# Two static pairs of experts at the head of a two-layer MoE encoder, and constants multiplied in the waits of each layer's last item

## The chip, the core and the metric

One core of one Trainium2 chip runs the whole program. The metric is the time of one execution on the device in microseconds (us). The engines are PE (TensorE), DVE (VectorE), ACT (ScalarE), POOL (GpSimd) and SP (SyncE, which here only issues DMAs). The rate of PE depends on the clock that is granted to it; in the records it is 1.00 (2.4 GHz) or 0.50 (1.2 GHz), and in between only as a mean over a stretch.

## What is computed

256 tokens of width 1024 go through two layers. Each layer is a mixer (one input projection, three kinds of attention, one output projection) and a mixture of experts: a router picks one of four groups and then two of the eight experts in it. All data is float32.

```python
def reference(x, ...):
    for l in range(DEPTH):                       # DEPTH = 2
        x = x + mixer_sublayer(x, ...)
        x = x + hier_moe(rms_norm(x, norm2_g[l]), ...)
...
    # hier_moe: 32 experts, D_EXPERT = 512, top-2 inside the best group
    e_in = jnp.take_along_axis(e_logits, grp[:, None, None], axis=1)[:, 0]
    top_v, top_i = lax.top_k(e_in, TOP_K_IN_GROUP)
    gate = p_grp[:, None] * jax.nn.softmax(top_v, axis=-1)
...
        return (jax.nn.silu(xb @ w_gate[e]) * (xb @ w_up[e])) @ w_down[e]
```

Every expert has tokens for these inputs, so all 32 experts' weights (6 MB each) are read in both layers. The reference's router, run on these inputs, gives experts 28 to 31 the counts 5, 12, 6, 1 in the first layer and 1, 33, 13, 8 in the second; the largest counts of the others are 54, 42, 35, 31, 28 and 73, 56, 44, 40, 27.

## The kernel before, in words

**The ring.** All large weights pass through `ring`, 16 pieces of 1 MB. `ring_plan` (L86) gives each transfer its piece in advance, one after the other around the ring, and the semaphore value that frees it. A layer's `w_in` takes nine pieces in three groups, `w_out` four, an expert six: two each of gate, up and down. SP issues transfers strictly in the program's order (`piece_in`, L397 to L403) and waits at each one until its piece is free.

**Items.** The 32 experts of a layer are worked on in 11 items of 1, 2 or 4 experts (`KINDS`, in the order of rank; `TIME` is the order in which they are worked on). An item of four gives each expert 32 places of the 128 columns, one of two gives 64, one of one 128. Experts 30 and 31 are `STATIC`: they form the first item whatever the router says. The others are ranked by their number of tokens, and their numbers stand in `order`, which DVE writes (L1514). At every item but the first SP waits for `v_order` (L465). Tokens that don't fit the places of an expert's rank are done again in `rerun`, which loads six pieces more for each.

**An item on PE.** A gather (L847), which makes `xg` from `pick`; six rounds (`round_of`, L878: gate 0 and 1, up 0 and 1, down 0 and 1), each of which frees its pieces at its end by `p_round` or `p_down`; small transposes (L916, L930); and four products back (L947) that DVE adds to `x` (L1617). DVE copies the first half of the gathered rows (`v_xg`, L1561), ACT the second half (`a_xg`, L1144); round 0 needs the first half, round 1 the second. The next item's gather stands between round 3 and round 4. Each layer's last item gathers at its start, and its last transfers are split by rows (`row_in`, L405 to L411), so that its last round (L895) can begin with the first half; the second half waits for `d_last`. Between rounds 4 and 5 of the last item stand seven products of constants (`warm`, L592), whose result nobody reads.

**The head of a layer's experts.** After the logits (L755) PE multiplies constants three times and waits for `v_chosen`. DVE finds the two best experts of each token (L1441 to L1466); PE counts them with `ones` and `tri` (L839); DVE makes the order of the experts (L1496 to L1514), then the places of the static pair (`placings`, L1476 on) and `pick` (L1572), for which the gather waits. After it follow `seatings` (the places of all experts) and `list_again`.

**The mixer.** PE, DVE, ACT and POOL work through a written order of projections, scores, softmax and products. Near the middle PE turns the queries of kind B (L672) after `v_sum`, which DVE writes at L1332; ahead of that DVE reduces the lengths of these queries (L1242) and copies a turned softmax (L1328).

## Time and profile before

| | us |
|---|---|
| median of three runs | 1226.13 (1226.09 to 1231.55) |
| the profiled execution | 1228.69 |
| its span in the trace | 1226.9 |
| mixer of the first layer | 0 to 150 |
| experts of the first layer | 150 to 621 |
| mixer of the second layer | 621 to 755 |
| experts of the second layer | 755 to 1223 |
| busy: PE, DVE, ACT, POOL | 1007.5, 321.6, 169.4, 51.5 |

A row of a timeline begins with its start and its duration in us; then come the engine, the line, the operation, the tiles written and read, and the number of instructions. What stands in brackets is the engine's idle time before it and what ended that. A row of windows has, for each stretch, the busy time of each engine with its number of instructions, the granted clock of PE, the mean busy share of the 16 DMA engines and what they moved in GB/s. A product in float32 shows as two instructions.

### The profile page before, as it was taken

The numbers are of one execution on the slowest core, as the hardware profiler recorded it, in microseconds if no ns is written. First come the engines' busy times: TensorE is split into PE (matmuls) and PEld (weight loads), VectorE is DVE, ScalarE is ACT, GpSimd is POOL, SyncE is SP. The second block draws the span as 40 slices with busy tenths as digits, with TensorE's granted clock in tenths as the row PEclk, the third lists the DMA queues.
The fourth block names the chain that finished last, engine by engine and source line by source line (L and its number), as shares of the span: only waits on it lengthen the run. The fifth ranks groups of instructions, "written<-read, shape, count | busy, mean of one in ns | idle before, by whom it ended". The sixth has DMA issues, their size and how long they took to land.

```text
span 1226.9 us, 14093 instructions
## 1 busy us (share of the span) xinstructions
PE 1007.5 (82%) x5416; PEld 472.2 (38%) x5416; DVE 321.6 (26%) x727; ACT 169.4 (14%) x440; POOL 51.5 (4%) x104
## 2 busy tenths in 40 slices
PE   7999899887969659657799998979889696795667
PEld 4565553333423223213256655434334241241232
DVE  3555542221212102102045555412212021020101
ACT  1343311010100001000024332101011010010000
POOL 1121100000000000000021110000000000000000
PEclk9999999998999888888899998999899897798888
DMA  9942099999999999999988222999999999999996
GB/s 299 371 183 103 1 374 408 421 421 421 421 421 421 422 420 392 406 422 420 412 321 332 100 97 94 399 412 420 421 420 422 421 420 421 421 421 422 420 420 244
DMA packets 74820, 435.84 MB, mean 355 GB/s; under 512 B 12496, under 2 KB 15744, under 8 KB 26624
## 3 DMA queue, kind: packets, MB, share of 16 engines
q1 hardware_dynamic: 74752, 434.92, 87.1%
q8 instruction: 45, 0.74, 0.2%
q14 instruction: 23, 0.19, 0.0%
HBM read 433.84 MB, written 1.05 MB: 354 GB/s over the span
## 4 chain that ended last, share of the span: by engine, by line
PE 52%; DMA 33%; SPq 8%; issue 2%; DVE 2%; ACT 2%; POOL 1%; DVEq 0%; ACTq 0%; POOLq 0%
PE bank L878 23%; DMA ring<-in_w_down 22%; PE bank L624 9%; DMA ring<-in_w_up 7%; SPq L403 6%; PE bank L740 5%; PE bank L947 4%; DMA ring<-in_w_gate 4%; PE bank L847 4%; PE bank L708 1%; PE bank L696 1%; PE bank L686 1%; SPq L411 1%; ACT work L1144 1%; DMA ring<-in_w_in 1%
## 5 line engine op out<-in xcount | busy, mean ns | idle before, releaser
L878 PE MATMUL bank<-ring,work 128*32 128x512 f32 (+2 forms) x3008 | 529.2, 688 | 184.3 <-DMA ring<-in_w_up 68.3
L878 PEld LDWEIGHTS bank<-ring,work 128*32 128x32 f32 (+2 forms) x3008 | 162.3, 134 | 513.6 <-issue 485.4
L624 PE MATMUL bank<-ring,hT 128*128 128x512 f32 (+1 forms) x384 | 130.3, 495 | 1.1 <-DMA ring<-in_w_in 1.1
L847 PE MATMUL bank<-work,h 128*128 128x128 f32 x704 | 92.6, 295 | 11.8 <-issue 6.6
L847 PEld LDWEIGHTS bank<-work,h 128*128 128x128 f32 x704 | 89.4, 209 | 27.3 <-issue 20.2
L1612 DVE COPY work<-bank 128x512 f32<-128x512 f32 x22 | 15.2, 691 | 311.5 <-PE bank L878 278.7
L624 PEld LDWEIGHTS bank<-ring,hT 128*128 128x128 f32 x384 | 72.8, 194 | 49.6 <-issue 42.8
L1604 DVE TENSOR_TENSOR work<-work,bank 128x512 f32<-128x512 f32 x22 | 15.1, 687 | 256.2 <-PE bank L878 256.2
L947 PE MATMUL bank<-work 128*128 128x512 f32 x176 | 82.0, 607 | 0.0
L1617 DVE TENSOR_TENSOR x<-x,bank 128x512 f32<-128x512 f32 x88 | 60.5, 688 | 19.2 <-PE bank L947 19.2
L1144 ACT ACTIVATE work<-bank,gain 128x128 f32<-128x128 f32 x88 | 25.1, 367 | 272.3 <-PE bank L847 272.3
L740 PE MATMUL bank<-ring,h 128*128 128x512 f32 x128 | 59.2, 606 | 0.0
L947 PEld LDWEIGHTS bank<-work 128*128 128x128 f32 x176 | 30.1, 189 | 51.8 <-issue 38.4
L1155 ACT COPY work<-bank 128x256 f32<-128x256 f32 x22 | 8.2, 372 | 290.5 <-PE bank L916 290.5
L1586 DVE TENSOR_TENSOR work<-iota,work 128x512 f32<-128x512 f32 x20 | 13.8, 690 | 126.4 <-PE bank L916 124.9
L1166 ACT COPY work<-bank 128x512 f32<-128x512 f32 x22 | 12.9, 585 | 215.7 <-PE bank L878 186.7
L740 PEld LDWEIGHTS bank<-ring,h 128*128 128x128 f32 x128 | 23.4, 193 | 24.8 <-issue 24.6
L512 POOL TENSOR_TENSOR ms<-ms,eps 128x1 f32<-128x1 f32 x20 | 3.8, 192 | 588.6 <-ACT h L995 500.3
L1342 DVE SCALAR_TENSOR_TENSOR x<-bank,rstd,x 128x512 f32<-128x512 f32 x24 | 18.0, 750 | 33.7 <-PE bank L740 33.7
L1164 ACT COPY work<-bank 128x512 f32<-128x512 f32 x22 | 13.2, 599 | 78.4 <-PE bank L930 78.4
L1561 DVE TENSOR_TENSOR work<-bank,gain 128x512 f32<-128x512 f32 x22 | 15.2, 691 | 31.7 <-PE bank L847 31.7
L515 POOL TENSOR_TENSOR rsh<-msh,mhalf 128x8 f32<-128x8 f32 (+1 forms) x14 | 22.0, 1568 | 1.1
(192 smaller groups left out, 588.5 us busy)
## 6 DMA issues: line engine op xcount, KB each, us to landing
ring<-in_w_gate SPq DMA_DIRECT2D x128, 1024.0 KB, 26.2
ring<-in_w_up SPq DMA_DIRECT2D x128, 1024.0 KB, 26.6
ring<-in_w_down SPq DMA_DIRECT2D x120, 1024.0 KB, 25.3
ring<-in_w_in SPq DMA_DIRECT2D x10, 1536.0 KB, 13.2
ring<-in_w_out SPq DMA_DIRECT2D x8, 1024.0 KB, 17.7
ring<-in_w_down SPq DMA_DIRECT2D x16, 512.0 KB, 20.5
ring<-in_w_in SPq DMA_DIRECT2D x1, 2048.0 KB, 14.7
x<-in_x SPq DMA_DIRECT2D x2, 512.0 KB, 4.6
```

What stands on the lines that cost most here:

```text
L403: sp.dma_start(rows(pos, k), w[:, 0, half * k:half * k + k]).then_inc(landed[pos], 16)
L515: tt(dst, src, spread_to(mhalf, src), ALU.pow).then_inc(g_rstd, 1)
L624: last = matmul(bank[6 + i % 2][:, 0:c1 - c0], hT[:, k, t * P:t * P + P], group_in(l, gi)[:, k, c0:c1], start=(k == 0), stop=(k == KD - 1))
L740: last = matmul(bank[6 + n % 2][:, :], mixed[:, pos0 + c, t * P:t * P + P], rows(pos, 2)[:, c % 2, half * 512:half * 512 + 512], start=(c ...
L847: last = nc.tensor.matmul(bank[k // 4][:, k % 4 * P:k % 4 * P + P], h_kc[:, t, k, :], pick[:, t, :], start=(t == 0), stop=(t == TT - 1))
L878: last = nc.tensor.matmul(bank[b][e * w:e * w + w, :], lhs[:, k, e * w:e * w + w], rows(pos, k_count // 2)[:, kk, n * 512:n * 512 + 512], ...
L947: last = nc.tensor.matmul(bank[2 + n][:, :], pickT[:, t, :], y[:, half * 512:half * 512 + 512], start=True, stop=True)
L1144: last = nc.scalar.mul(xg[:, k, :], bank[1][:, (k - 4) * P:(k - 3) * P], gain2[:, q // NI, k:k + 1])
L1342: stt(xs, bank[6 + n % 2][:, :], rstd[:, c:c + 1], xs, ALU.mult, ALU.add).then_inc(v_x, 1)
L1561: tt(xg[:, 0:4, :], bank[0][:, :].rearrange("p (k s) -> p k s", k=4), wide(gain2[:, q // NI, 0:4], P), ALU.mult).then_inc(v_xg, 1)
L1612: nc.vector.tensor_copy(y[:, 512:1024], bank[7][:, :]).then_inc(v_y, 1)
L1617: tt(xs, xs, bank[2 + n][:, :], ALU.add).then_inc(v_back[n], 1)
```

## The change

1. `STATIC` is 28 to 31, and `KINDS` begins 2, 2, 1, 1: the first two items are static pairs, ahead of any order. `TIME` puts the second pair right behind the first. The two items of one expert come fourth and sixth. The places of each rank move by two with the statics, in `seatings`.
2. `ring_plan` takes the piece that is freed earliest and no longer goes around the ring. Five places beside the ring are laid out (`BESIDE`) in memory that is free while experts are worked on, but `BESIDE_LAST = -1` lets no item use them. For this, tables are moved together, `c_dil` is loaded in each layer, and SP gets waits for these places. `hot` takes over the space of `hotw` and `beats`, so `seatings` counts ranks in two halves.
3. The places of the static pair are made ahead of the order, and PE counts with `tri` first.
4. Round 0 waits for `v_xg` alone, `a_xg` is waited for ahead of round 1.
5. Constants are multiplied (three times at the head of the program, five in place of three behind the logits, 5, 5, 5 and 4 behind rounds 0 to 3 of the last item, two ahead of `d_last`); the seven behind round 4 go.
6. In the mixer, DVE's reduction of the lengths of B's queries is moved behind the copy and `v_sum`. Squares of the last two groups of heads go to other memory, and ACT's waits for `p_sum` there go.

```diff
-STATIC = (30, 31)
-KINDS = [2, 1, 1, 2, 2] + [4] * 6
+STATIC = (28, 29, 30, 31)
+KINDS = [2, 2, 1, 1, 2] + [4] * 6
...
-TIME = [0, 5, 1, 6, 2, 7, 3, 8, 4, 9, 10]
+TIME = [0, 1, 5, 2, 6, 3, 7, 4, 8, 9, 10]
...
+    def take(key, n, done, time, allowed):
+        starts = [i for i in allowed if i + n <= max(allowed) + 1 or n == 1]
+        pos = min(starts, key=lambda i: (max(when[i:i + n]), i))
...
+                if l:
+                    dil_load(l)
...
-                if i:
+                if r0 >= NS:
                     sp.wait_ge(v_order, 2 * l + 1 + (r0 + n > 16))
...
-                warm(7, 3)
+                warm(7, 5)
                 pe.wait_ge(v_chosen, l + 1)
...
                         if kk == 1:
+                            warm(2, 2)
                             pe.wait_ge(d_last, 16 * n_e * (l + 1))
...
                 pe.wait_ge(v_xg, q + 1)
-                pe.wait_ge(a_xg, q + 1)
                 need(pe, v_back[0], q)
                 round_of(0, (2,), xg, p_round)
+                if i == NI - 1:
+                    warm(7, 5)
+                pe.wait_ge(a_xg, q + 1)
                 round_of(1, (2,), xg, p_round)
+                if i == NI - 1:
+                    warm(7, 5)
...
                 round_of(2, (3,), xg, p_round)
+                if i == NI - 1:
+                    warm(7, 5)
                 round_of(3, (3,), xg, p_round)
+                if i == NI - 1:
+                    warm(7, 4)
...
                 round_of(4, (6, 7), hidT, p_round)
-                if i == NI - 1:
-                    warm(2, 7)
...
                 projected(l, 11)
-                head_lengths(l, "qB")
                 softmax_copied(l, 4)
                 sum_raised(l, 1)
+                head_lengths(l, "qB")
...
-                expert_order(l)
                 placings(l)
                 seated(nc.vector.tensor_copy(rgc[:, 0:TT], rg[:, 0:TT, e0:e0 + 2]))
                 tt(pair_hot, ...).then_inc(v_pick, 1)
+                expert_order(l)
                 expert_order_rest(l)
...
-                seated(tt(hotw, hot, wide(weights, P), ALU.mult))
-                tt(pickw, hotw[:, 0:TT], hotw[:, TT:], ALU.add).then_inc(v_pickw, 1)
+                dve.wait_ge(v_pick, q + 1)
+                seated(tt(hot, hot, wide(weights, P), ALU.mult))
+                tt(pickw, hot[:, 0:TT], hot[:, TT:], ALU.add).then_inc(v_pickw, 1)
```

DVE at the head of the experts, before; `bank` holds PE's counts, `order` the experts' numbers, and `work` is, among others, `pick`:

```order
L1496 SCALAR_TENSOR_TENSOR work<-bank,order_key 128x32 [waits p_rank]
L1508 MAX work<-work 1x8 [waits v_step]
L1509 MATCH_REPLACE work<-work 1x32 [waits v_step]
L1510 MAX work<-work 1x8 [waits v_step]
L1514 TENSOR_SCALAR order<-work 1x16 [waits v_step]
L1476 SCALAR_TENSOR_TENSOR work<-bank,work 128x2x32 [waits v_chosen,p_rank]
L1478 TENSOR_SCALAR rg<-work 128x64 [waits v_step]
L1571 COPY rgc<-rg 128x4 [waits v_step]
L1572 TENSOR_TENSOR work<-iota,rgc 128x256 [waits v_istep]
```

and the same place now:

```order
L1528 SCALAR_TENSOR_TENSOR work<-bank,work 128x2x32 [waits v_chosen,p_rank]
L1530 TENSOR_SCALAR rg<-work 128x64 [waits v_step]
L1623 COPY rgc<-rg 128x4 [waits v_step]
L1624 TENSOR_TENSOR work<-iota,rgc 128x256 [waits v_istep]
L1548 SCALAR_TENSOR_TENSOR work<-bank,order_key 128x32 [waits p_rank]
L1560 MAX work<-work 1x8 [waits v_step]
```

The five instructions that make the order now stand behind the write of `pick`.

PE at the end of the last item of the second layer, from round 3 on, before (`ring,work 32x512` are the rounds, `dil,ident` the constants, `work 128x512` the products back):

```order
L878 MATMUL bank<-ring,work 32x512 [waits landed0,landed1,landed15,landed14]
L878 MATMUL bank<-ring,work 32x512 x15
L930 MATMUL bank<-ident,work 128x128 [waits v_back2,v_hid]
L930 MATMUL bank<-ident,work 128x128 x3
L878 MATMUL bank<-ring,work 32x512 [waits landed3,landed2,landed4,v_y,landed5,a_y,a_hidT]
L878 MATMUL bank<-ring,work 32x512 x15
L592 MATMUL bank<-dil,ident 128x384 x7
L895 MATMUL bank<-ring,work 32x512 [waits landed8,landed9,landed7,landed6]
L895 MATMUL bank<-ring,work 32x512 x7
L895 MATMUL bank<-ring,work 32x512 [waits d_last]
L895 MATMUL bank<-ring,work 32x512 x7
L947 MATMUL bank<-work 128x512 [waits a_y,a_pickT]
```

and now:

```order
L923 MATMUL bank<-ring,work 32x512 [waits landed10,landed11,landed5,landed4]
L923 MATMUL bank<-ring,work 32x512 x15
L631 MATMUL bank<-ident 128x384 x4
L984 MATMUL bank<-ident,work 128x128 [waits v_back2,v_hid]
L984 MATMUL bank<-ident,work 128x128 x3
L923 MATMUL bank<-ring,work 32x512 [waits landed6,landed0,landed12,v_y,landed13,a_y,a_hidT]
L923 MATMUL bank<-ring,work 32x512 x15
L941 MATMUL bank<-ring,work 32x512 [waits landed8,landed14,landed7,landed1]
L941 MATMUL bank<-ring,work 32x512 x7
L631 MATMUL bank<-ident 128x384 x2
L941 MATMUL bank<-ring,work 32x512 [waits d_last]
L941 MATMUL bank<-ring,work 32x512 x7
```

The seven products of constants behind round 4 are gone; four stand behind round 3 and two ahead of the second half of the last round.

In the first layer the ring is filled, before and now, by the static pair's 12 transfers, of which nine wait for the projections' `p_proj`. The four pieces left are those of `w_out`, freed by `p_out` 4, 4, 8 and 12. Before, they go to the gate 0 weights of an item of four, behind `v_order`; now to gate 0 and gate 1 of the second static pair. The next transfer waits for `p_round` 1, the end of the first item's round 0, in both kernels.

## Rows read from the trace of the kernel before

**Rows 1.** The page: granted clock in tenths and DMA rate, 40 equal slices

```profile
PEclk9999999998999888888899998999899897798888
GB/s 299 371 183 103 1 374 408 421 421 421 421 421 421 422 420 392 406 422 420 412 321 332 100 97 94 399 412 420 421 420 422 421 420 421 421 421 422 420 420 244
```

**Rows 2.** SP's waits: us in total, times, longest

```profile
SPq L465 <- DVE order L1514: 107.1, 2, 54.4
```

**Rows 3.** Windows of the first layer: engines, clock, DMA share, GB/s

```profile
110.00:150.00 40.00, 38.75 (x193) 22.70 (x191) 21.10 (x59) 15.48 (x35) 4.90 (x13) 1.00 0.00 1
...
165.00:170.00 5.00, 5.00 (x24) 1.73 (x22) 4.37 (x23) 1.14 (x2) 0.00 (x0) 1.00 0.82 280
...
185.00:190.00 5.00, 5.00 (x22) 1.65 (x17) 1.15 (x2) 0.58 (x1) 0.00 (x0) 1.00 0.98 387
...
195.00:200.00 5.00, 5.00 (x50) 1.53 (x46) 0.51 (x1) 0.51 (x2) 0.00 (x0) 1.00 0.98 377
```

**Rows 4.** Timeline of PE, first item and start of the second, first layer

```profile
153.69 6.38 PE L847 MATMUL bank<-work,h 128*128 128x128 f32 x32 [2.38 <-DVE work L1572]
161.34 7.09 PE L878 MATMUL bank<-ring,work 128*64 128x512 f32 x32 [1.28 <-issue]
...
175.75 3.84 PE L847 MATMUL bank<-work,h 128*128 128x128 f32 x32
...
192.01 7.07 PE L878 MATMUL bank<-ring,work 128*32 128x512 f32 x64
```

**Rows 5.** Timeline of all engines, head of the first layer's experts

```profile
151.42 0.18 DVE L1496 SCALAR_TENSOR_TENSOR work<-bank,order_key 128x32 f32<-128x32 f32 x1
...
152.43 0.22 DVE L1476 SCALAR_TENSOR_TENSOR work<-bank,work 128x64 f32<-128x64 f32 x1
...
160.10 1.14 ACT L1144 ACTIVATE work<-bank,gain 128x128 f32<-128x128 f32 x4 [8.27 <-PE bank L847]
```

**Rows 6.** Timeline of PE, head of the second layer's experts

```profile
752.30 3.50 PE L592 MATMUL bank<-dil,ident 128*128 128x384 f32 x6
...
758.61 5.44 PE L847 MATMUL bank<-work,h 128*128 128x128 f32 x32 [2.31 <-issue]
```

**Rows 7.** Timeline around the turn of B's queries, both layers

```profile
97.03 1.09 PE L696 MATMUL bank<-ident,work 128*128 128x128 f32 x8 [0.19 <-DVE work L1321]
...
99.06 0.69 DVE L1242 TENSOR_REDUCE msh<-work 128x8 f32<-128x512 f32 x1 [1.69 <-ACT work L1021]
...
100.55 0.63 PE L672 MATMUL bank<-ident,h 128*128 128x128 f32 x4 [2.09 <-DVE ms L1332]
...
707.10 0.63 PE L672 MATMUL bank<-ident,h 128*128 128x128 f32 x4 [2.09 <-DVE ms L1332]
```

**Rows 8.** Windows in which the clock fell

```profile
753.10:756.40 3.30, 3.02 (x10) 1.16 (x8) 2.96 (x24) 1.36 (x1) 0.00 (x0) 0.50 0.00 0
...
101.60:104.80 3.20, 3.20 (x17) 2.04 (x16) 0.07 (x1) 1.10 (x4) 1.31 (x4) 0.55 1.00 425
```

**Rows 9.** Timeline of PE, end of the second layer

```profile
1194.71 6.32 PE L878 MATMUL bank<-ring,work 128*32 128x512 f32 x32 [6.33 <-DMA ring<-in_w_up]
...
1204.64 6.47 PE L878 MATMUL bank<-ring,work 128*32 128x512 f32 x32 [1.98 <-DMA ring<-in_w_down]
1211.04 4.78 PE L592 MATMUL bank<-dil,ident 128*128 128x384 f32 x14
1215.75 3.64 PE L895 MATMUL bank<-ring,work 128*32 128x512 f32 x32
```

**Rows 10.** Window in which the weights' last bytes come

```profile
1214.00:1214.50 0.50, 0.50 (x3) 0.32 (x2) 0.00 (x0) 0.00 (x0) 0.00 (x0) 1.00 0.02 8
```

**Rows 11.** Timeline of PE, last item of the first layer

```profile
574.44 7.07 PE L878 MATMUL bank<-ring,work 128*32 128x512 f32 x64 [1.28 <-issue]
...
603.69 3.64 PE L878 MATMUL bank<-ring,work 128*32 128x512 f32 x32 [1.40 <-DMA ring<-in_w_down]
...
615.42 1.92 PE L895 MATMUL bank<-ring,work 128*32 128x512 f32 x16 [1.53 <-DMA ring<-in_w_down]
```

More of the change, by code:

```diff
@@ L83 @@
 OUT_PIECES = (2, 3, 0, 1)
+BESIDE_FREE = [("p_pv", 8, 24)] * 4 + [("p_logit", 2, 40)]
+TABLES, BIASES, TURNED_ROWS = PIECES + 2, PIECES + 3, PIECES + 4
+BESIDE_LAST = -1
 def ring_plan():
-    at, used, freed, plan = [0], [0] * PIECES, [[] for _ in range(PIECES)], {}
-    def take(key, n, done):
-        if at[0] + n > PIECES:
-            at[0] = 0
-        pos = at[0]
-        before = [f for i in range(pos, pos + n) for f in freed[i]]
+    n_pieces = PIECES + BESIDE
+    used, freed, when, plan = [0] * n_pieces, [None] * n_pieces, [0] * n_pieces, {}
+    def take(key, n, done, time, allowed):
+        starts = [i for i in allowed if i + n <= max(allowed) + 1 or n == 1]
+        pos = min(starts, key=lambda i: (max(when[i:i + n]), i))
         waits = {}
-        for name, value in before:
+        for name, value in filter(None, freed[pos:pos + n]):
             waits[name] = max(value, waits.get(name, 0))
@@ L101, in take @@
             used[i] += i < pos + 2
-            freed[i] = [done]
+            freed[i], when[i] = done, time
         plan[key] = (pos, [used[i] for i in range(pos, pos + n)], sorted(waits.items()))
-        at[0] = (pos + n) % PIECES
+    ring, everything = range(PIECES), range(n_pieces)
     for l in range(LAYERS):
+        t0 = 1000 * l
         for g in range(3):
-            take((l, "in", g), 3, ("p_proj", 12 * l + 4 * g + 4))
+            take((l, "in", g), 3, ("p_proj", 12 * l + 4 * g + 4), t0 + 4 * g + 4, ring)
         for n, j in enumerate(OUT_PIECES):
-            take((l, "out", j), 1, ("p_out", 12 * l + (4, 4, 8, 12)[n]))
+            take((l, "out", j), 1, ("p_out", 12 * l + (4, 4, 8, 12)[n]), t0 + (16, 16, 26, 30)[n], ring)
+        for n, (name, count, time) in enumerate(BESIDE_FREE):
+            freed[PIECES + n], when[PIECES + n] = (name, (l + 1) * count), t0 + time
         for i, it in enumerate(TIME):
@@ L115, in ring_plan @@
                 for e in range(KINDS[it]):
-                    take((l, i, r, e), 1, done)
+                    take((l, i, r, e), 1, done, t0 + 100 + 10 * i + r, everything if i <= BESIDE_LAST else ring)
+        for n in range(BESIDE):
+            plan[l, "beside", PIECES + n] = freed[PIECES + n]
     return plan
@@ L215, in encoder @@
                    "kB": proj[:, :, 256:512], "qB": proj[:, :, 256:512]}
[L216 to L220 removed]
+        staged = [queries.rearrange("p j s -> p (j s)"), hT_flat]
+        flip = [s[0:GRID, 0:P] for s in staged]
+        windows = [s[0:GRID, P:P + 1000] for s in staged]
+        gain_rows = [s[0:3 * KD, 1128:1128 + P] for s in staged]
+        beside = [work[:, 0:PIECE], work[:, PIECE:2 * PIECE], tables[:], biased[:], hT_flat]
+        o = [2 * PIECE]
         def carve(n):
@@ L257, in encoder @@
             sem("d_" + n) for n in ("ident", "gains", "rel", "mask", "rope", "qkg", "route", "gain2", "const", "out"))
-        d_last = sem("d_last")
-        landed = [sem(f"landed{i}") for i in range(PIECES)]
+        d_last, d_dil = sem("d_last"), sem("d_dil")
+        landed = [sem(f"landed{i}") for i in range(PIECES + BESIDE)]
         p_gains, p_xT, p_proj, p_flip, p_turn, p_s, p_pt, p_pv, p_sum, p_out, p_yT, p_logit, p_rank = (
@@ L290, in rows @@
         def rows(pos, k):
-            return ring[:, pos * PIECE:(pos + 1) * PIECE].rearrange("p (k c) -> p k c", k=k)
+            piece = ring[:, pos * PIECE:(pos + 1) * PIECE] if pos < PIECES else beside[pos - PIECES]
+            return piece.rearrange("p (k c) -> p k c", k=k)
         def rooted(l, name):
@@ L361, in spread, with kept_no_more, dil_load @@
                 return src.partition_broadcast(P).rearrange("p a c -> p (a c)")
+            def kept_no_more(l, pos):
+                name, value = PLAN[l, "beside", pos]
+                sp.wait_ge(frees[name], value)
+            def dil_load(l):
+                if l:
+                    kept_no_more(l - 1, TABLES)
+                sp.dma_start(dil, a["c_dil"]).then_inc(d_dil, 16)
             def staged_loads(l):
+                kept_no_more(l - 1, TURNED_ROWS)
                 gain_loads(l)
@@ L1428, in mixers @@
                 if l == 0:
[L1429 removed]
+                    dve.wait_ge(d_const, 64)
                     router_constants()
```

104 lines of the change are left out of this document (57 added, 47 removed).

## The prediction

> **What bounds the kernel now.** I read the page's slices first [rows 1]: in each layer the stream of weights runs at 421 GB/s for about 450 us, and idle in the second half of the mixer. A piece of 1.049 MB at 421 GB/s takes 2.49 us, so a layer's 192 pieces of experts' weights take 478 us; everything that starts this stream earlier, or shortens what follows its last byte, counts in full, and most of what PE does in between is hidden. SP's own waits come next: 107.1 us go to waiting for the order of the experts, twice some 54 us [rows 2], and that wait looks like what the change removes. The windows then show where the stream leaves gaps: none of it runs from 110 to 150 us, and once running it dips to 280 GB/s at 165 to 170 us and slightly at 185 and 195 [rows 3]. Last come the timelines of PE at the head of the experts and at the end of each layer, which say what the stream and the end wait for.
>
> **The two static pairs.** It is tempting to count four pieces more per layer ahead of the order, 4 x 2.49 = 10.0 us a layer. But the ring holds 16 pieces before and now. Before, 12 lie ready and four are fetched from 153.6 us on, which takes until about 165; the 17th needs the piece that round 0 of the first item frees. That round starts at 161.34 and is half of the two rounds' 7.09 us [rows 4], so it ends at 164.9. The dip at 165 to 170 [rows 3] is this: the stream has caught up with PE and waits for it. Now all 16 lie ready and the stream resumes with the 17th, released by the same round. From there both streams run off the start of round 0, T0. So the head start itself is worth nothing; only a shift of T0 is.
>
> Then the pace. An item costs PE 192.01 - 161.34 = 30.7 us whether it has two experts or four [rows 4], since 64 or 32 columns of several experts run side by side. The first static pair frees two pieces at T0 + 3.6, 7.1, 11.0, 14.5, 23.6 and 27.1, the second at 30.7 more each. The stream needs 2.49 us a piece: 24 pieces take 59.8 us, and with a gap each where the pair of pieces comes late (behind the products back of either item) I get 61.5, a loss of 1.7 us. Before, the item of four follows, and the two dips behind the 17th piece cost (421 - 387) x 5 / 421 + (421 - 377) x 5 / 421 = 0.9 us [rows 3]. The change loses 0.8 us here in the first layer; in the second I take 0.2, as the same dips were deeper there. PE does not starve: the second pair's up weights are in 10 us after T0, it asks for them after 38. Later the items of one expert free only six pieces in 30.7 us where the stream wants 12, but the item of four before them leaves some 13 pieces free ahead, so they cost nothing.
>
> **T0.** (a) `pick` is written ahead of the order: five DVE instructions from 151.42 to 152.43 leave its path, 1.0 us [rows 5]. They then run during the gather, and end before DVE is wanted for the first half of it. (b) Round 0 no longer waits for ACT's half, 1.28 us of PE's idle time behind the gather [rows 4, 5]; round 1 wants it 3.5 us later, and 1.14 us suffice. (c) The first gather runs at the low clock, 6.38 us where the next takes 3.84 [rows 4]; in the second layer 5.44 [rows 6]. Five products of constants instead of three end at about 151.0, when the counts can start, and (a) shortens the wait behind them to 1.3 us. I take the full clock in the first layer, 2.5 us, with 0 as the other end. In the second the clock had fallen while the products still ran: six instructions took 3.50 us, and the window shows 0.50 with PE busy 3.02 of 3.30 us [rows 6, 8]. There two more products may run at half rate and hold up the counts by up to 2 us, against a gather faster by 1.6: I take +0.6, between -0.5 and +1.6. T0 moves by 1.0 + 1.3 + 2.5 = 4.8 and by 1.0 + 1.3 + 0.6 = 2.9 us. Together with the loss above: 4.0 and 2.7 us.
>
> The Trainium skill ("TensorE: Matmul & The Clock Gate", Part 4: PE-mode transpose) says that transposes don't count as activity for the clock as other products do; the fall behind the turned rows in the second layer agrees, and the first layer, with the same sequence and no fall until 152 us, does not. If the rule held each time, (c) would be the low end in both layers.
>
> **The mixer.** DVE stands idle for 1.69 us, reduces lengths from 99.06, then copies, then writes `v_sum`, and PE stands 2.09 us until 100.55 [rows 7]. The copy can start at 98.1, when PE's turned softmax is out (97.03 + 1.09), so `v_sum` is there at about 98.95 and PE goes on at 99.1: 1.45 us. The same in the second layer [rows 7]. The lengths come out as before, at 99.75, since they wait for ACT until 99.0 in any case. In the first layer the clock then stood at 0.55 for 3.2 us of full work [rows 8], which costs 3.2 x 0.45 = 1.4 us; with the idle time more than halved I count it as won (0 is the other end). PE is busy 38.75 of the 40 us that follow [rows 3], so this reaches T0. ACT's dropped waits were for sums long made: nothing. The three products at the head lie in waits for `x` and `w_in`: 0, at most 0.1 us lost.
>
> **Extra work.** `c_dil` is loaded again in the second layer, 0.8 MB or 1.9 us of a DMA queue that then stands empty for 70 us [rows 1]; SP's new waits are for values long reached. `seatings` has two DVE instructions more, with the next gather 14 us behind T0 and, by my count of DVE's rows, done some 2.5 us ahead of it: hidden, and 1 us late at worst. No expert overflows: 28 to 31 have at most 33 tokens for 64 places, the two largest others 54 and 73 for 128, the next two at most 44 for 64, the rest 28 or fewer for 32.
>
> **The ends of the layers.** At the end of the second layer round 4 starts at 1204.64 at half rate and takes 6.47 us, seven constants 4.7, and only at 1215.75 does the last round of 3.64 us begin; its second half begins at 1217.6 [rows 9]. The last bytes are in at 1214.5 [rows 10]. Now round 4 at full clock ends at 1208.3, the first half and two constants at 1212.7, and the second half can begin as the rows land: 3.1 us won. In the first layer the second half waits for its data at 615.42 already [rows 11]: nothing. For this the item must keep up: from 574.44 - 1.28, four rounds (14.2), 19 constants at 0.68 (12.9), the biases and turns (5) and ACT's copy end at about 606.5, past the 603.69 of before, then round 4, the half and two constants end at 613.5, 2 us ahead of the data [rows 11]. In the second layer the biases are missing, and the slack is some 5 us.
>
> **Sum.** First layer 1.45 + 1.4 + 4.0 = 6.9; second 1.45 + 2.7 + 3.1 = 7.2; together 14 us. The profiled execution would be 1228.7 - 14 = 1214.7; the medians stand 2.6 us below it, so 1226.1 - 14 = 1212 us.
>
> **The rivals.**
> - *The clock stays low.* In (c) and the mixer no clock is won (-2.5, -1.1, -1.4), and at the ends PE still cools in the waits: half rate over the second half and the products back costs up to 3.4 us in each layer, if some 3.4 of their 1.9 + 3.7 us run at it. That leaves 14 - 5 - 6.8 = 2, so 1224. For it: rounds at half rate behind 6.3 us of idle time [rows 9]. Against: the constants fill 3.4 us of such a wait. Here also belongs the skill's rule (same page, Part 1, HAM oscillation) that a stream whose work is shorter than its waits for data cools at every step; rows 9 agree with it for the kernel before.
> - *Slower: the constants become the last item's bound.* If the last item runs at half rate, its 19 constants cost 1.4 us each and its rounds 7, so its chain grows by up to 32 us against a slack of 2 to 5. It decides from some 4 us at half rate in the first layer on; with half of the item slow, 13 us are lost in each layer: 1212 + 26 = 1238. Against: 0.5 came after idle time, and rounds that followed each other ran at 1.00.
> - *The head start counts in full,* if the stream didn't depend on round 0: some 8.6 us a layer on top, 1195. The dip in rows 3 speaks against it.
>
> **How the numbers follow.** Forecast, 1206 to 1219: 0.74. Clock stays low, 1219 to 1226: 0.17. Slower: 0.05. Full head start: 0.04. The range 1205 to 1221 leaves out about 2 in 10. A measurement can tell 0.5%, 6.1 us, from no change: faster (below 1220) 0.80, same 0.14, slower 0.06.
>
> **What would show it.** SP's wait for the order gone, but a wait for PE's first round in its place and a stream that is idle until 3.6 us behind T0; T0 at about 153.5 in the first layer (161.34 - 4.8 - 2.9 from the mixer) and the gather at 3.8 us; PE's idle time at L672's successor down to 0.6 us; round 4 of the last item at 3.6 us; the second half of the last round released by DMA in both layers. It is wrong if the stream resumes earlier than round 0's end, if the gathers still take 5 to 6 us, or if `d_last` is long met when PE comes to it.

## The result, and the profile after

The changed kernel takes 1215.15 us (median of four runs, 1211.87 to 1216.72) against 1226.11 us for the kernel before in the same comparison. The ratio is 0.9896 with a 95% interval of [0.9874, 0.9918], so it is faster by 0.8 to 1.3%. The profiled execution took 1214.72 us with a span of 1212.9, 14.0 less than the span before.

The page of the kernel after: granted clock and DMA rate in 40 slices, to be read against [rows 1].

```profile
PEclk9999899999998988788999999998998989888799
...
GB/s 303 379 180 135 108 306 401 415 421 421 421 422 420 421 423 387 408 422 420 413 325 367 104 173 71 393 403 420 423 420 421 421 421 421 421 420 422 420 420 286
```

The fifth slice shows 108 in place of 1: the second pair's four pieces now come in the middle of the mixer. The next slices show no rate above that of before. SP's waits in the kernel after (in all, times, longest) answer to [rows 2]; the last line is the same wait in the kernel before:

```profile
SPq L439 <- PE bank L923: 271.8, 87, 20.4
...
SPq L439 <- PE bank L780: 79.6, 6, 21.2
...
SPq L403 <- PE bank L878: 209.5, 78, 9.2
```

The 107 us of waiting for the order are gone, and SP waits longer for PE's rounds instead: 271.8 us at L923 against 209.5 us before. Windows of the first layer, T0 (the start of the first item's round 0) being 154.22, answer to [rows 3]; the last line is a row of SP's timeline, its transfers from 157.91 on:

```profile
150.00:155.00 5.00, 4.52 (x36) 3.99 (x38) 4.41 (x26) 0.67 (x3) 0.00 (x0) 1.00 0.00 0
155.00:160.00 5.00, 5.00 (x26) 1.72 (x24) 4.62 (x15) 0.47 (x2) 0.00 (x0) 1.00 0.22 43
160.00:165.00 5.00, 5.00 (x26) 1.55 (x22) 4.35 (x25) 2.25 (x3) 0.00 (x0) 1.00 1.00 423
...
175.00:180.00 5.00, 5.00 (x26) 1.72 (x24) 0.00 (x0) 0.35 (x1) 0.00 (x0) 1.00 1.03 397
...
157.91 4.24 SPq L439 DMA_DIRECT2D ring<-in_w_up  x4
```

The ring is full and the stream stands still until the first item's round 0 ends: the first piece behind it is issued at 157.91, 3.7 us after T0. PE at the head of the program and in the first layer's mixer and head, against [rows 4, 7]:

```profile
10.69 7.14 PE L664 MATMUL bank<-ring,hT 128*128 128x256 f32 x32 [0.31 <-DVE hT L1261]
...
97.09 0.63 PE L712 MATMUL bank<-ident,h 128*128 128x128 f32 x4 [0.60 <-DVE ms L1384]
...
140.50 2.58 PE L795 MATMUL bank<-w_route,hT 128*128 128x36 f32 x16 [0.77 <-ACT hT L1127]
142.90 6.22 PE L631 MATMUL bank<-ident 128*128 128x384 f32 x10
148.95 0.20 PE L884 MATMUL bank<-work,tri 128*128 128x32 bf16 x2
...
150.48 3.81 PE L892 MATMUL bank<-work,h 128*128 128x128 f32 x32 [1.25 <-DVE work L1624]
154.22 7.09 PE L923 MATMUL bank<-ring,work 128*64 128x512 f32 x32
```

T0 moved from 161.34 to 154.22. The gather is at full speed and round 0 follows without idle time. But the constants took 6.22 us for ten instructions, where the same ten take 3.47 in the second layer, and the counts (L884) had to wait for them. The same place of the first layer in the kernel before, where PE waited 1.50 us for DVE ahead of the counts:

```profile
145.56 1.95 PE L755 MATMUL bank<-w_route,hT 128*128 128x36 f32 x16 [0.77 <-ACT hT L1077]
147.34 2.18 PE L592 MATMUL bank<-dil,ident 128*128 128x384 f32 x6
151.01 0.21 PE L839 MATMUL bank<-work,ones 128*128 128x32 bf16 x2 [1.50 <-DVE work L1466]
```

From the start of the last logits to the counts it was 5.45 us before and is 8.45 us now, so 3.0 us are lost there. The second layer, against [rows 6, 7]:

```profile
699.37 0.63 PE L712 MATMUL bank<-ident,h 128*128 128x128 f32 x4 [0.60 <-DVE ms L1384]
...
744.56 3.47 PE L631 MATMUL bank<-ident 128*128 128x384 f32 x10
748.24 0.22 PE L884 MATMUL bank<-work,tri 128*128 128x32 bf16 x2 [0.21 <-DVE work L1518]
749.86 3.81 PE L892 MATMUL bank<-work,h 128*128 128x128 f32 x32 [1.32 <-DVE work L1624]
753.60 7.09 PE L923 MATMUL bank<-ring,work 128*64 128x512 f32 x32
```

The end of the second layer on PE, against [rows 9]:

```profile
1193.47 5.04 PE L923 MATMUL bank<-ring,work 128*32 128x512 f32 x32 [3.05 <-DMA ring<-in_w_down]
1198.59 1.92 PE L941 MATMUL bank<-ring,work 128*32 128x512 f32 x16
1200.45 1.56 PE L631 MATMUL bank<-ident 128*128 128x384 f32 x4
1203.49 1.92 PE L941 MATMUL bank<-ring,work 128*32 128x512 f32 x16 [1.48 <-DMA ring<-in_w_down]
1205.35 3.72 PE L999 MATMUL bank<-work 128*128 128x512 f32 x8
```

The second half of the last round now waits for its data. Cut at four marks of each layer (the turn of B's queries, the last logits, T0, the last products back), the 14.0 us lie here, in us, second layer behind the slash:

| stretch | before | after | won | predicted |
|---|---|---|---|---|
| start, or last products back, to the turn, less its idle time | 98.46 / 87.72 | 96.49 / 87.72 | 1.97 / 0 | 0 / 0 |
| idle time at the turn | 2.09 / 2.09 | 0.60 / 0.60 | 1.49 / 1.49 | 1.45 / 1.45 |
| turn to logits | 45.01 / 43.42 | 43.41 / 43.41 | 1.60 / 0 | 1.4 / 0 |
| logits to T0 | 15.78 / 14.80 | 13.72 / 10.82 | 2.06 / 3.98 | 4.8 / 2.9 |
| T0 to the last products back | 455.95 / 454.01 | 456.83 / 451.75 | -0.88 / 2.26 | -0.8 / 2.9 |

The sums are 14.0 measured and 14.1 predicted. Two of the ten terms are off by 2 to 2.7 us, in opposite directions, and two more by 1.1 and 0.6, so the agreement of the sums is in part luck. The experiments say which terms belong to the change and which to one execution.

### The profile page after: what moved, and what is told of

It reads as the page before. It is cut to its first block, busy times and chain, and to the rows that moved or that the text cites. A ratio compares the mean times of both kernels' runs of the same rounds, so it can differ in the third digit from the quotient of the medians.

```text
span 1212.9 us, 14196 instructions
## 1 busy us (share of the span) xinstructions
PE 1014.6 (84%) x5488; PEld 474.2 (39%) x5488; DVE 324.1 (27%) x735; ACT 169.6 (14%) x440; POOL 51.4 (4%) x104
## 4 chain that ended last, share of the span: by engine, by line
PE 58%; DMA 29%; SPq 8%; DVE 2%; ACT 1%; issue 1%; POOL 1%; DVEq 0%; ACTq 0%; POOLq 0%
PE bank L923 27%; DMA ring<-in_w_down 19%; PE bank L664 9%; PE bank L999 5%; PE bank L780 5%; PE bank L892 5%; DMA ring<-in_w_up 4%; DMA ring<-in_w_gate 4%; SPq L439 4%; SPq L447 2%; PE bank L736 1%; PE bank L748 1%; PE bank L631 1%; PE bank L726 1%; DMA work<-in_c_flip 1%
## 5 line engine op out<-in xcount | busy, mean ns | idle before, releaser
L923 PE MATMUL bank<-ring,work 128*32 128x512 f32 (+2 forms) x3008 | 518.8, 672 | 173.2 <-DMA ring<-in_w_down 66.0
L923 PEld LDWEIGHTS bank<-ring,work 128*32 128x32 f32 (+2 forms) x3008 | 158.1, 132 | 495.7 <-issue 467.2
L892 PE MATMUL bank<-work,h 128*128 128x128 f32 x704 | 86.8, 283 | 7.6 <-DVE work L1640 5.1
L892 PEld LDWEIGHTS bank<-work,h 128*128 128x128 f32 x704 | 83.5, 197 | 23.1 <-issue 16.4
L631 PE MATMUL bank<-ident 128*128 128x384 f32 x112 | 44.4, 543 | 2.7 <-DMA ident<-in_c_ident 2.7
L631 PEld LDWEIGHTS bank<-ident 128*128 128x128 f32 x112 | 22.2, 210 | 23.6 <-issue 14.1
```

What stands on the lines that cost most here:

```text
L631: matmul(bank[b][:, 0:3 * P].rearrange("p (n s) -> p n s", n=3), ident[:], ident[:].unsqueeze(1).broadcast_to([P, 3, P]), start=True, stop ...
L892: last = nc.tensor.matmul(bank[k // 4][:, k % 4 * P:k % 4 * P + P], h_kc[:, t, k, :], pick[:, t, :], start=(t == 0), stop=(t == TT - 1))
L923: last = nc.tensor.matmul(bank[b][e * w:e * w + w, :], lhs[:, k, e * w:e * w + w], rows(pos, k_count // 2)[:, kk, n * 512:n * 512 + 512], ...
```

## The experiments

Each kernel was timed beside the kernel before. Medians of the kernel before were 1227.9, 1226.0 and 1226.6 us in the three comparisons, so the ratios are what to compare; 0.001 of ratio is 1.2 us.

### The pairs alone

Changes 1 and 2 without the rest: round 0's wait, the constants, DVE's order of instructions at the head and in the mixer are those of before. PE's counting with `tri` first and the other memory for squares stay as in the kernel after. Against the kernel before, in part:

```diff
-STATIC = (30, 31)
-KINDS = [2, 1, 1, 2, 2] + [4] * 6
+STATIC = (28, 29, 30, 31)
+KINDS = [2, 2, 1, 1, 2] + [4] * 6
...
-TIME = [0, 5, 1, 6, 2, 7, 3, 8, 4, 9, 10]
+TIME = [0, 1, 5, 2, 6, 3, 7, 4, 8, 9, 10]
```

The diffs of all other experiments are against the kernel after.

> The opposite: two static pairs and the ring plan of the change, but the constants, the order ahead of the places, the wait for both halves of the gathered rows and the lengths ahead of the copy as before the change. Theory A and B: the first round starts where it did, and the stream ran off it before already: the same as the kernel before or up to 1.6 us slower, 1226 to 1228. Theory C: 17 us faster than before, near 1209.

Measured: 1229.77 us (10 runs), ratio 1.0016 [0.9997, 1.0035]. T0 was at 161.07 and 765.38, as before:

```profile
153.53 6.27 PE L887 MATMUL bank<-work,h 128*128 128x128 f32 x32 [2.38 <-DVE work L1613]
...
161.07 7.09 PE L918 MATMUL bank<-ring,work 128*64 128x512 f32 x32 [1.28 <-issue]
```

What the change is named after brings nothing by itself. The full head start (the third rival) is refuted for a ring of 16 pieces.

### One pair, with everything else of the change

```diff
-STATIC = (28, 29, 30, 31)
-KINDS = [2, 2, 1, 1, 2] + [4] * 6
-TIME = [0, 1, 5, 2, 6, 3, 7, 4, 8, 9, 10]
+STATIC = (30, 31)
+KINDS = [2, 1, 1, 2, 2] + [4] * 6
+TIME = [0, 5, 1, 6, 2, 7, 3, 8, 4, 9, 10]
```

> The changed kernel with one static pair (experts 30 and 31) and the old order of the items; all other edits stay. Theory A (the trace of the changed kernel): without the second pair the stream's next four pieces wait for the order, which is ready some 3 us ahead of the first round; they then take 10 us, so the 17th piece starts about 10.2 us behind the start of round 0 and no longer 5.5 us. That costs 4.7 us a layer less the 0.8 us of pace won back: 6 to 9 us slower than the changed kernel, near 1222. Theory B (the recorded prediction taken literally, the head start is worth nothing by itself): 0 to 1.6 us faster than the changed kernel. Theory C (the four pieces count in full): 17 to 20 us slower, near 1233.

Measured: 1218.36 us (4 runs), ratio 0.9921 [0.9892, 0.9951], so 3 us slower than the kernel after, though the two intervals overlap. The trace has a place for it. T0 was at 155.87, and SP issued the first transfer that needs the order here; the second line is the same place in the kernel before:

```profile
154.05 9.95 SPq L439 DMA_DIRECT2D ring<-in_w_gate  x8
...
153.56 15.89 SPq L403 DMA_DIRECT2D ring<-in_w_gate  x8
```

Before, the order came 7.7 us ahead of T0 (161.34), and four pieces were in the ring by the time that round 0 ended. Now it comes 1.8 us ahead of T0, since `pick` overtakes it and the gather is shorter, and one pair can no longer fill the ring in time. From T0 to the last products back this run took 457.7 and 453.5 us; six with two pairs and the same last items (the kernel after, and the five below that keep 16 places and change something else) took 456.1 and 452.0 in mean (454.6 to 456.9 and 451.6 to 452.7). So the second pair is worth some 1.5 us a layer, but only once T0 has moved; one execution with one pair stands behind this. All three theories missed that: it is less than A said and more than B said.

### Five places beside the ring, for two items and for nine

```diff
-BESIDE_LAST = -1
+BESIDE_LAST = 1
```

and in the second kernel

```diff
-BESIDE_LAST = -1
+BESIDE_LAST = 8
```

> The changed kernel, in which items 0 and 1 may also use the five places beside the ring (21 places, BESIDE_LAST = 1). Theory A: when the second pair is done, at some 61 us behind the first round, the stream can be no further than the 24 consumed pieces and the 16 of the ring, where it is now already, since both run at PE's pace: the same as the changed kernel within 1.5 us. Theory C (what lies ready at the first round counts): five pieces, 12 us a layer, 24 us faster, near 1191.

> The changed kernel with the five places open to all items but the last two (BESIDE_LAST = 8), so that the ring has 21 places through most of a layer. Theory A: the stream is five pieces further ahead at the end of the second pair and stays there until the last two items, where the ring is 16 again; with PE up to 14 pieces behind it, the lead is kept: 10 to 12 us a layer, near 1192 to 1195. Rival: the lead is given back where the places close, since the last two items must wait for ring pieces that PE frees: within 3 us of the changed kernel.

Measured: 1210.27 us (4 runs), ratio 0.9867 [0.9833, 0.9901], with the places open to the first two items; 1188.08 us (4 runs), ratio 0.9664 [0.9633, 0.9695], with them open to the first nine. By the ratios the second is 28 us faster than the kernel after and 41 faster than the kernel before, the fastest of all, and a little more than its theory A's 10 to 12 us a layer. The first is 3.6 us faster than the kernel after by the ratios, with overlapping intervals; from T0 to the last products back it took 454.0 and 450.5 us, 2.1 and 1.6 less than the mean above. That is more than its theory A gave, and far from theory C's 24. Windows of the first kernel, T0 150.30:

```profile
180.00:190.00 10.00, 10.00 (x45) 3.23 (x45) 2.89 (x6) 0.87 (x2) 0.00 (x0) 1.00 1.01 401
190.00:200.00 10.00, 9.69 (x62) 5.71 (x58) 2.15 (x4) 0.69 (x3) 0.00 (x0) 1.00 0.51 183
200.00:210.00 10.00, 9.03 (x37) 3.17 (x38) 1.38 (x2) 1.51 (x4) 0.00 (x0) 1.00 0.66 215
```

Five pieces are ahead at T0, but when the stream is back on 16 places it waits at 183 and 215 GB/s until PE has caught up. A head start lasts only as long as the room that holds it.

### One pair and five places: the square completed

The diff is that of the one pair, with `BESIDE_LAST = 8`.

> The kernel after with one static pair (30 and 31, items in the order of before) and with the five places beside the ring open to the first nine items of a layer. It completes a square: two pairs with 16 places (1215 us), one pair with 16 (1218), two pairs with 21 (1188). Theory A (pairs and places are worth something only together: the second pair can be fetched ahead of the order only where there is room, and the room can be filled ahead of it only with weights known in advance; 21 places less 16 are 5 pieces of 2.49 us, 12.5 us a layer): at T0 only 12 pieces are in the ring and none beside it, SP issues the rest behind the order as with 16 places, the stream already ran at 413 to 422 GB/s from there on with 16, so 1216 to 1219 us, as with one pair and 16 places. Theory B (the room alone does it, since the stream waits for free pieces all along): about 1191, 27 us faster than with 16. Between them, about 1205, if half of the gain comes from waits later in the layer.

Measured: 1219.35 us (10 runs), ratio 0.9941 [0.9923, 0.996]. The square, in ratios to the kernel before:

| | 16 places | 21 places |
|---|---|---|
| one pair | 0.9921 | 0.9941 |
| two pairs | 0.9896 | 0.9664 |

Room alone is worth nothing, the second pair alone 3 us, both together 31 us. Windows ahead of T0 show the mechanism. Two pairs and 21 places (T0 155.27):

```profile
140.00:150.00 10.00, 9.23 (x48) 6.76 (x48) 4.91 (x27) 6.12 (x7) 0.74 (x2) 0.83 0.78 300
150.00:160.00 10.00, 8.75 (x60) 5.46 (x60) 8.80 (x37) 1.14 (x4) 0.00 (x0) 1.00 0.03 6
```

One pair and 21 places (T0 155.42):

```profile
140.00:150.00 10.00, 9.23 (x51) 7.07 (x50) 5.03 (x27) 6.13 (x7) 0.74 (x2) 0.83 0.00 0
150.00:160.00 10.00, 8.75 (x60) 5.46 (x60) 8.68 (x37) 1.14 (x4) 0.00 (x0) 1.00 0.54 193
```

and SP's wait in the latter, with its first transfer behind it:

```profile
SPq L504 <- DVE order L1566: 107.0, 2, 53.5
...
153.60 1.49 SPq L439 DMA_DIRECT2D ring<-in_w_gate  x2
```

PE's busy times are alike to the tenth. The first kernel has its weights moved before 150; the second issues the first of them at 153.60, 1.8 us ahead of T0. From T0 to the last products back the first kernel took 441.6 and 440.0 us, 14.5 and 12.1 less than the mean above. Five pieces of 2.49 us are 12.5.

### No constants at the head of the program

```diff
-                    warm(6, 2)
...
-                if l == 0:
-                    warm(6, 1)
...
-                if l == 0:
-                    warm(6, 1)
```

> The kernel after without the three products of constants at the head of the program; all else as in the kernel after. The first projections took 32 instructions of 9.28 us before and 7.14 after. Theory A (the constants keep the clock up in the waits for x and w_in): the projections go back to 9.2 to 9.3 us, B's turn comes 2.0 us later, and so does everything behind it: time and span +2.0 us against the kernel after, whatever the mixer's own gains. Theory B (my prediction: the products are worth nothing, the 2 us have another cause, such as when the rows arrive): projections stay at about 7.1 us, time +0 us.

Measured: 1213.80 us (4 runs), ratio 0.9905 [0.9882, 0.9929], the same as the kernel after. The projections ran at full speed without them:

```profile
11.12 7.14 PE L664 MATMUL bank<-ring,hT 128*128 128x256 f32 x32 [1.77 <-DMA ring<-in_w_in]
```

Over all profiles, the three others without these constants took 9.02 to 9.28 us for this row and all ten with them 7.14; but with them the clock fell later in several, as at 20 to 30 us in the kernel with the last item as before (0.66). Counted to the turn, less the 1.49 us of idle time where it still stood, ten executions with the constants needed 96.0 to 101.8 us, 98.8 in mean, and four without 97.9 to 99.1, 98.7 in mean. So they are worth nothing that can be measured, and the 1.97 us that the profiled kernel after won here are one execution's clock.

### The lengths of B's queries first

```diff
+                head_lengths(l, "qB")
                 softmax_copied(l, 4)
                 sum_raised(l, 1)
-                head_lengths(l, "qB")
```

> The kernel after with the reduction of B's lengths back ahead of the copy and v_sum, in both layers. Theory A (this order alone makes PE's idle time at the turn of B's queries): idle 2.1 us again in place of 0.6, 1.5 us later in each layer, total +3 us; if the idle time also brings the clock down in the first layer, another 1.4 us, total +4.4. Theory B (the shorter idle time came from something else, the head constants say): idle stays near 0.6, time +0.

Measured: 1218.47 us (4 runs), ratio 0.9934 [0.991, 0.9959], 4.7 us slower than the kernel after. PE at the turn in the first layer:

```profile
98.02 0.63 PE L712 MATMUL bank<-ident,h 128*128 128x128 f32 x4 [2.09 <-DVE ms L1384]
98.58 1.94 PE L748 MATMUL bank<-work 128*64 128x128 f32 x16
```

The idle time is back, and the 16 products behind it take 1.94 us where they take 1.09 at full clock. From turn to logits this kernel needed 45.04 and 46.27 us. Over all profiles: with 2.09 us of idle time 44.9 to 46.3 in five stretches of six, and 43.4 in one; with 0.60 us 43.4 in all 22. Theory A holds, and the clock's part is larger than its 1.4 us: it appeared in both layers.

### The last item's constants as before

```diff
                         if kk == 1:
-                            warm(2, 2)
                             pe.wait_ge(d_last, 16 * n_e * (l + 1))
...
                 round_of(0, (2,), xg, p_round)
-                if i == NI - 1:
-                    warm(7, 5)
...
                 round_of(1, (2,), xg, p_round)
-                if i == NI - 1:
-                    warm(7, 5)
...
                 round_of(2, (3,), xg, p_round)
-                if i == NI - 1:
-                    warm(7, 5)
                 round_of(3, (3,), xg, p_round)
-                if i == NI - 1:
-                    warm(7, 4)
...
                 round_of(4, (6, 7), hidT, p_round)
+                if i == NI - 1:
+                    warm(2, 7)
```

> The kernel after with the last item's constants as in the kernel before: seven behind round 4, none behind rounds 0 to 3 and none ahead of d_last. Theory A (PE cools in the last item's waits of the second layer): round 4 there takes 6.3 to 6.5 us at half rate again, the last round's second half begins late behind PE and not at the data, +3.1 us in the second layer, 0 in the first, total +3. Theory B (my first rival turned round: the constants already hold the item up, in the first layer above all): the first layer's end comes earlier than in the kernel after, by up to 2 us. Theory C (round 4 at full rate without them, since the waits are shorter now): +0.

Measured: 1218.77 us (5 runs, 1214.14 to 1219.53), ratio 0.9926 [0.99, 0.9952]. PE at the end of the second layer, T0 755.71:

```profile
1195.60 5.34 PE L923 MATMUL bank<-ring,work 128*32 128x512 f32 x32 [2.99 <-DMA ring<-in_w_down]
1200.87 4.78 PE L631 MATMUL bank<-ident 128*128 128x384 f32 x14
1205.58 3.64 PE L940 MATMUL bank<-ring,work 128*32 128x512 f32 x32
```

The second half began 451.7 us after T0 (1205.58 + 1.82), in the kernel after 449.9: 1.8 us in place of 3.1, since round 4 took 5.34 us and not 6.47. So theory A holds at a part of its size. In the first layer the last products back came 455.9 us after T0 and 456.8 in the kernel after, but the six kernels with the constants spread from 454.6 to 456.9, so theory B's cost is not shown. The traces of the kernel after and the kernel before speak against it: the stream ran at 418 to 424 GB/s from 565 to 595 us in both, and in all six the second half of the last round waited 0.5 to 1.7 us for its data and not for the constants. The rest of this kernel's difference lies ahead of its last items (its turn was at 101.83), so its median says little on them.

### All constants as before

The edits are those of the kernels without head constants and with the last item as before, together, and `warm(7, 3)` in place of `warm(7, 5)` behind the logits.

> The kernel after with all constants as in the kernel before: none at the head, three behind the logits, the last item's seven behind round 4. Theory A (the constants bring what the separate parts say): head +2.0, second layer's end +3.1, the first layer's gather at low clock again (6.3 in place of 3.8) +2.5, the second layer's gather 5.4 in place of 3.8 but counts earlier, +0.6: together +8.2 us against the kernel after. Theory B (five constants at low clock behind the logits of the first layer hold up the counts by the 2.4 us seen there, so that three are as good as five): head +2.0 and end +3.1 alone, +5 us. Theory C: the constants bring nothing together and all of the gain is in the order of instructions: +0 to 1.

Measured: 1217.96 us (6 runs), ratio 0.9932 [0.991, 0.9955], 4.4 us slower than the kernel after, nearest to theory B's 5. From T0 to the last products back 456.2 and 454.1 us; gathers of 6.64 and 3.81.

### Both halves of the gathered rows ahead of round 0

```diff
                 pe.wait_ge(v_xg, q + 1)
+                pe.wait_ge(a_xg, q + 1)
                 need(pe, v_back[0], q)
```

> The kernel after with ACT's half of the gathered rows waited for ahead of round 0 again, in every item. Theory A (term b of the prediction): 1.28 us of idle time between gather and round 0 in each layer's first item; at full clock 12.1 us from the logits to T0 in place of 10.85; together +2.6 us, plus up to 1.3 us at either end where the last item is late. Theory B (round 1 waited for ACT anyway, so the idle time had only moved one round on): T0 later by 1.28 but the start of round 2 no later than in the kernel after, total +0.

Measured: 1217.34 us (4 runs), ratio 0.9922 [0.9897, 0.9948], 3.2 us slower. The idle time stands ahead of round 0 again, in both layers, and nothing behind gives it back:

```profile
157.19 7.09 PE L923 MATMUL bank<-ring,work 128*64 128x512 f32 x32 [1.28 <-issue]
```

### The order ahead of `pick`

```diff
+                expert_order(l)
                 placings(l)
...
                 seated(nc.vector.tensor_copy(rgc[:, 0:TT], ...))
                 tt(pair_hot, ...).then_inc(v_pick, 1)
-                expert_order(l)
```

> The kernel after with the order of the experts written ahead of the places of the first pair on DVE, as in the kernel before. Theory A (term a): PE's wait ahead of the gather 2.2 to 2.4 us in place of 1.25 to 1.37, from the logits to T0 11.85 us in place of 10.85 at full clock, +1.0 in each layer, together +2. Theory B (my range's other side: behind `pick` the five instructions delay DVE's first half of the gathered rows by as much as they win): from the logits to T0 10.85 as before, +0.

Measured: 1220.00 us (7 runs), ratio 0.9944 [0.9926, 0.9962], 5.9 us slower. Logits to T0 took 14.75 and 16.35 us, more than either theory said, because the clock went with the wait:

```profile
151.88 0.20 PE L884 MATMUL bank<-work,tri 128*128 128x32 bf16 x2
...
154.47 5.44 PE L892 MATMUL bank<-work,h 128*128 128x128 f32 x32 [2.32 <-DVE work L1625]
```

1.07 us more of waiting, and 1.63 us more of gather behind five constants, in both layers.

### Three constants behind the logits

```diff
-                warm(7, 5)
+                warm(7, 3)
                 pe.wait_ge(v_chosen, l + 1)
```

> The kernel after with three products of constants behind the logits in place of five. In the profiles so far five products ran at full clock (3.47 us) in 8 stretches and slower (5.1 to 6.2) in 6, and every gather behind them took 3.81; with three, 5 of 6 gathers took 5.4 to 6.6. Theory A (three leave PE idle long enough for the clock to fall): the gathers take 5.4 to 6.6 us in both layers, from the logits to T0 13.4 us in place of 10.85, +2.5 in each layer; against the profiled kernel after, whose first layer lost 2.9 us in the constants themselves, -0.3 there and +2.6 in the second. Theory B (with the shorter wait of the new order on DVE three suffice, as in the second layer of the run with all constants as before): gathers 3.81, 10.85 in both layers, -2.9 in the first layer against the profiled kernel after and 0 in the second.

Measured: 1213.38 us (5 runs), ratio 0.9908 [0.9877, 0.9939], the same as the kernel after. The gathers were slow, as theory A said:

```profile
147.99 5.44 PE L892 MATMUL bank<-work,h 128*128 128x128 f32 x32 [1.37 <-DVE work L1624]
...
746.75 5.27 PE L892 MATMUL bank<-work,h 128*128 128x128 f32 x32 [1.33 <-DVE work L1624]
```

Yet logits to T0 took 12.5 and 12.3 us, not 13.4: at full clock the three constants leave the counts waiting for DVE only, and a gather at the lower clock costs 1.5 to 1.6 us here. The stretch from logits to T0 over all kernels, mean of the layers' stretches:

| behind the logits | stretches | mean us | gathers of 3.81 us |
|---|---|---|---|
| as before (3 constants, order first, both halves) | 4 | 15.4 | 0 |
| 3 constants, `pick` first, first half only | 4 | 12.3 | 1 |
| 5 constants, `pick` first, first half only | 16 | 11.8 (10.8 to 13.7) | 16 |
| 5 constants, order first, first half only | 2 | 15.6 | 0 |

The 16 and the two are the same PE instructions; what differs ahead of the gather is 2.3 us of waiting against 1.2 to 1.4. With three constants PE also waits 1.5 us ahead of the counts, in six stretches of eight. Over all 28 stretches, those with both halves and five constants included, the two waits add up to 1.2 to 1.6 us in the 19 with a gather of 3.81 us, and to 2.3 to 3.9 us in the nine with a slower one.

## Why the prediction was right, and where it was not

The forecast of 1212 us (1205 to 1221) stands beside 1215.15 us, and the direction with its bound (faster than 1220) was right.

**The ring.** Right, and shown from both sides: the pairs alone give nothing, and five more places give 12 to 14.5 us a layer. The stream resumed at T0 + 3.7, where 3.6 was forecast. What the step missed is that moving `pick` ahead of the order and shortening the gather bring the order closer to T0, 1.8 us instead of 7.7, so that the second pair is needed to keep the ring full. "Only a shift of T0" was right for two pairs; with one pair it would have cost some 1.5 us a layer. The pace loss in the first layer, 0.88 for 0.8, is less sure than it looks: over six kernels that share the code of this stretch it took 454.6 to 456.9 us, against 455.95 in the kernel before.

**(a) and (b).** Right: 1.07 and 1.28 us in both layers, each shown by undoing it.

**(c), the gather's clock.** The step that failed for the first layer. It took the constants' own time as fixed and put the clock's loss in the gather. In the profiled execution the clock had fallen in the logits already (2.58 us against 1.95), the ten instructions took 6.22 us, and 3.0 us were lost ahead of the counts, more than the 2.6 us that the gather won; the stretch from logits to T0 won 2.06 in place of 4.8. That T0 still came at 154.22, near the 153.6 that the terms add up to, is luck: the 1.97 us won at the start of the program were in no term. In the second layer, where half rate was feared, they ran at full clock and 3.98 came in place of 2.9. The low end in the text, where two more products at half rate hold up the counts, is what happened, but in the other layer. In the mean of 16 stretches (11.8 us, against 15.4 in the four as before) a layer wins 3.6 us, of which 2.35 are (a) and (b) and 1.25 the clock: 2.5 us for two layers, where 3.1 were put down. Of the 1.25, five constants in place of three explain only some 0.5; the rest came with the shorter wait for `pick`.

The Trainium skill's rule on transposes ("TensorE: Matmul & The Clock Gate", Part 4: PE-mode transpose) foresees a fall behind the turned rows. With five constants behind the logits, 12 stretches of 20 agree (4.9 to 6.3 us for the ten instructions) and 8 do not (3.47), so it named a risk and not an outcome.

**The mixer.** Right in mechanism: 1.49 us of idle time less in both layers of every profile with the new order (22 stretches). The clock behind it was counted once, in the first layer; the six stretches with the longer idle time lost 1.5 us in mean over both layers, so it was undersized. The kernel before had full clock in the second layer by chance.

**The head products.** Costed at nothing, and right on the evidence of 14 executions, though the profiled pair alone shows 1.97 us and would have made it look like a missed term.

**The last items.** The mechanism was right, the half-rate round and the late second half; the size was 1.8 and 2.5 us in the two kernels with the constants taken back, not 3.1; round 4 took 5.34 and 6.40 us there. The sign that round 4 would take 3.6 us failed in the second layer of the kernel after, where it took 5.04; in the other five kernels with the constants it took 3.64 three times and 5.34 and 5.10. It stayed hidden, since the second half waited 1.48 us for its data all the same. Over six profiles with the constants and four without (the kernel before among them), the stretch from T0 to the last products back is 1.3 us shorter in the second layer (451.6 to 452.7 against 451.7 to 454.1) and 0.5 longer in the first, where the two sets overlap. The rival that the constants become the last item's bound is not borne out: they put off the start of round 4 in the first layer from 442.4 to 445.0 us behind T0, as the prediction had it, but the second half still waited for data. Of the rival of the low clock, the part at the ends did not come either: the second halves took 1.92 us and the products back 3.72, as at full clock.

**The medians.** They moved by 11 to 12.7 us (by difference and by ratio), less than the profiled pair's 14.0. The terms as the experiments have them, for two layers: mixer 3.0 of idle time and up to 3 of clock, head of the experts 7.2, last items 0.8, pace at most -1, products at the head of the program 0: 10 to 13. Which of the several clock falls an execution suffers is not settled, and no run here controls it.

## What to carry to other kernels

Before a head start is counted, ask what holds it: a transfer known earlier is worth the free places that it can fill, and a free place is worth the transfers known early enough to fill it; here the room alone gave nothing, the pair alone 0 to 3 us, and both 31. When an instruction is moved ahead of another, look at what the overtaken one releases, and how far that now stands from the point where it is needed. Cut two profiles at the same marks and compare the stretches over all kernels that share the code of a stretch: here a single pair of profiles showed 1.97 us at the start of the program that the change does not bring, and 1.5 us less ahead of the first T0 than it brings in the mean.

## What was not expected of the hardware

- The same PE instructions, behind the same waits, ran at different clocks from run to run: ten instructions of constants behind the logits took 3.47 us in 8 stretches and 4.9 to 6.3 in 12. The text on record for three constants counts 6 slower ones, those known then.
- One microsecond of waiting decided a lot: behind 1.2 to 1.4 us of waiting and five constants, all 18 gathers took 3.81 us; behind 2.3 us and the same constants, both took 5.44.
- The same instructions from the start to the turn of B's queries took 96.0 to 101.8 us, a spread as large as several of the effects studied here.
